# The norm chain of a two-block transformer: who sums the last squares, who takes the root, and how the result is spread

## The reference

```python
def rms_norm(x, g):
    xf = x.astype(jnp.float32)
    y = xf * lax.rsqrt(jnp.mean(xf * xf, axis=-1, keepdims=True) + EPS)
    return (y * g.astype(jnp.float32)).astype(x.dtype)
```

## Time and profile before

| what | us |
| --- | --- |
| runs | 2537.53, 2532.84, 2536.83 |
| profiled execution, its own time | 2532.73 |
| its span | 2530.9 |
| TensorE matmul busy | 2366.2 (93%) |
| VectorE busy | 1434.0 (57%) |
| ScalarE busy | 905.1 (36%) |
| GpSimd busy | 564.3 (22%) |
| mean granted clock of TensorE | 0.97 |

### The profile page before, as it was taken

The page is one execution under the profiler, slowest core; times in us unless marked ns, Lnnn a source line. Parts: engine busy times, 40 slices in busy tenths (PEclk is TensorE's granted clock), DMA queues, the critical chain, the costliest instruction groups (busy, mean ns, idle before and its releaser), DMA issues.

```text
span 2530.9 us, 29291 instructions
## 1 busy us (share of the span) xinstructions
PE 2366.2 (93%) x11174; PEld 1833.2 (72%) x11174; DVE 1434.0 (57%) x2277; ACT 905.1 (36%) x1539; POOL 564.3 (22%) x431
## 2 busy tenths in 40 slices
PE   6999999999998997888899999999899988999998
PEld 4665567888876864657788888888676566788886
DVE  4465547888757446665465566544636674534435
ACT  4244444232233223774332222222421773423232
POOL 2523114122211222002131211211123002322221
PEclk9999899999999999999899999999899999999999
DMA  5411114555521321001043334431122112222321
GB/s 185 150 53 42 55 34 175 200 179 188 175 79 34 107 67 52 27 22 47 30 133 123 127 128 132 127 103 62 50 89 83 34 34 67 84 92 92 102 90 50
DMA packets 77910, 234.06 MB, mean 92 GB/s; under 512 B 9215, under 2 KB 12416, under 8 KB 77772
## 3 DMA queue, kind: packets, MB, share of 16 engines
q1 hardware_dynamic: 70928, 217.48, 26.4%
q0 software_dynamic: 3520, 11.58, 1.3%
q10 hardware_dynamic: 3324, 3.14, 0.4%
HBM read 224.26 MB, written 7.90 MB: 92 GB/s over the span
## 4 chain that ended last, share of the span: by engine, by line
PE 86%; DVE 7%; ACT 3%; issue 2%; POOL 1%; ACTq 0%; DVEq 0%; POOLq 0%
PE psum L600 38%; PE psum L870 24%; PE psum L639 4%; PE psum L1168 3%; PE psum L1199 2%; PE psum L1125 2%; PE psum L659 2%; PE psum L1183 1%; PE psum L776 1%; PE psum L747 1%; PE psum L571 1%; PE psum L558 1%; PE psum L1139 1%; PE psum L1061 1%; DVE mla_stat L2007 1%
## 5 line engine op out<-in xcount | busy, mean ns | idle before, releaser
L600 PE MATMUL psum<-mix_split,weight_split 128*128 128x512 f32 x3792 | 786.7, 368 | 14.2 <-DVE mix_split L1316 5.9
L600 PEld LDWEIGHTS psum<-mix_split,weight_split 128*128 128x128 f32 x3792 | 651.0, 190 | 149.4 <-issue 17.7
L870 PE MATMUL psum<-hidden,weight_split 128*128 128x512 f32 (+1 forms) x3072 | 630.6, 366 | 0.0
L870 PEld LDWEIGHTS psum<-hidden,weight_split 128*128 128x128 f32 x3072 | 522.8, 188 | 104.4
L2086 ACT CAST weight_split<-weight_ring 128x1024 fp32r<-128x1024 f32 x269 | 276.8, 1040 | 301.2 <-PE psum L870 232.2
L2619 POOL TENSOR_TENSOR weight_split<-weight_ring,weight_split 128x1024 fp32r<-128x1024 f32 x89 | 233.9, 2628 | 541.3 <-ACT weight_split L2086 540.8
L1638 DVE TENSOR_TENSOR hidden<-hidden_tmp,hidden 128x512 fp32r<-128x512 f32 (+1 forms) x128 | 156.1, 1240 | 318.5 <-POOL hidden_tmp L2752 318.5
L2752 POOL TENSOR_TENSOR hidden_tmp<-hidden_tmp 128x512 f32<-128x512 f32 (+1 forms) x128 | 125.8, 994 | 615.1 <-ACT hidden L2331 614.9
L1262 DVE TENSOR_TENSOR weight_split<-weight_ring,weight_split 128x1024 fp32r<-128x1024 f32 x180 | 228.4, 1271 | 53.6 <-ACT weight_split L2086 53.6
L2327 ACT ACTIVATE hidden_tmp<-psum 128x512 f32<-128x512 f32 (+1 forms) x128 | 69.0, 539 | 494.9 <-PE psum L600 494.9
L600 PE MATMUL psum<-normed_in,weight_split 128*128 128x512 f32 (+1 forms) x1080 | 218.9, 364 | 9.0 <-DVE normed_in L1316 6.9
(11 more groups left out here) (303 smaller groups left out, 2415.6 us busy)
## 6 DMA issues: line engine op xcount, KB each, us to landing
weight_ring<-in_w_mlp SPq DMA_DIRECT2D x128, 512.0 KB, 3.8
weight_ring<-in_w_ff SPq DMA_DIRECT2D x64, 512.0 KB, 4.7
mod_ring<-in_w_mod SPq DMA_DIRECT2D x48, 512.0 KB, 3.8
late_ring<-in_w_mod SPq DMA_DIRECT2D x96, 256.0 KB, 3.5
weight_ring<-in_w_in SPq DMA_DIRECT2D x45, 512.0 KB, 3.7
weight_ring<-in_w_out SPq DMA_DIRECT2D x24, 512.0 KB, 3.6
weight_ring<-in_tables SPq DMA_DIRECT2D x13, 512.0 KB, 3.5
weight_ring<-in_w_v SPq DMA_DIRECT2D x8, 512.0 KB, 4.1
```

Of the source, the lines that this page charges most:

```text
L600: m = pe.matmul(psum[:, b + r, 0:hi - lo], w[:, part_w, :], x[:, part_x, k, lo:hi], start=k == 0 and part_w + part_x == 0, stop=k == KT - ...
L870: mm = pe.matmul(psum[:, b + r, 0:hi - lo], w[:, part_w, :], G[:, part_x, f % (2 * GROUP), lo:hi], start=jj == 0 and part_w + part_x == 0, ...
```

## The change

- The squares of the last tile are no longer added on VectorE. `column_sums` takes two matmuls for each 128 tokens, one on the sum of the first seven tiles and one on the last tile's squares, both into the same PSUM column. This holds for the norms in `LAST_APART`; `qn`, `kvn` and the context's part of `n3` sum as before.
- `mean` is gone: ScalarE's root reads the PSUM bank, with scale 1/n and EPS as bias. For `qn` the factor 1/sqrt(96) goes into scale and bias too.
- `diagonal` is gone: for each 128 tokens one matmul takes the column of inverses, repeated 128 times by an access pattern of step 0, as stationary operand, and the identity as moving one. The semaphore is raised after the fourth such matmul and after the last, and the first scaling of each range waits for its own.
- `n3` takes one root of ten columns: the product of the two norms' inverses is written as one root, of the gained mean plus EPS times the first mean plus EPS.
- ScalarE runs a root of one value where nothing waits (`root_table`), so that its table is loaded there.

The diff, without the edits that only pass the new arguments on:

```diff
+        LAST_APART = {"n1", "n2", "n3", "n3g", "l0n2", "l1n1", "l1n2", "fin"}
...
@@ -546,36 +549,43 @@
                 loads.append((name, index, width, split))
                 return i
-            def column_sums(tag, parts):
+            def column_sums(tag, parts, freed_by):
                 b = take()
                 bank_of[tag, "cols"] = b
                 wait_bank(b)
                 c = 0
-                for buf, lo, nt, name, key in parts:
-                    pe.wait_ge(*when(name, key))
+                for nt, planes in parts:
+                    for _, name, key in planes:
+                        pe.wait_ge(*when(name, key))
                     for t in range(nt):
-                        m = pe.matmul(psum[:, b, c:c + 1], buf[:, 0, lo + t * P:lo + (t + 1) * P], C["ones"][:, 0:1], start=True, stop=True)
-                        c += 1
+                        for n, (squares, _, _) in enumerate(planes):
+                            m = pe.matmul(psum[:, b, c + t:c + t + 1], squares[:, t * P:(t + 1) * P], C["ones"][:, 0:1], start=n == 0, stop=n == len(planes) - 1)
+                    c += nt
                 m.then_inc(*did(tag + "_pe", "cols"))
-                freed[b] = [(tag + "_vec", "mean")]
-            def on_all_partitions(tag, nt, diagonal=None, what="spread", diag="diag", n=2):
+                freed[b] = [freed_by]
+            def sums_and_last(tag, sums, last, lo, hi):
+                return (hi - lo) // P, [(sums[:, lo:hi], tag + "_vec", ("sum", KT - 2)), (last[:, lo:hi], tag + "_act", ("square", KT - 1))]
+            def on_all_partitions(tag, first, nt, what="spread", n=2):
                 b = take(n)
                 bank_of[tag, what] = b
                 wait_bank(*range(b, b + n))
-                pe.wait_ge(*when(tag + "_vec", diag))
-                src = SQ[:, 1, :] if diagonal is None else diagonal
-                for a in range(0, nt * P, 512):
-                    z = min(a + 512, nt * P)
-                    m = pe.matmul(bank(b, z, n)[:, a:z], C["ones"][:, :], src[:, a:z], start=True, stop=True)
-                m.then_inc(*did(tag + "_pe", what))
+                pe.wait_ge(*when(tag + "_vec", "inverse"))
+                for t in range(nt):
+                    m = pe.matmul(bank(b, nt * P, n)[:, t * P:(t + 1) * P], rs[:, first + t:first + t + 1].broadcast_to([P, P]), C["ident"][:, :], start=True, stop=True)
+                    if t % 4 == 3 or t == nt - 1:
+                        m.then_inc(*did(tag + "_pe", (what, t // 4)))
                 return b
-            def norm(tag, lo, nt, name, key, last):
-                column_sums(tag, [(SQ, lo, nt, name, key)])
-                b = on_all_partitions(tag, nt)
+            def norm(tag, nt, last, squares=None):
+                column_sums(tag, [sums_and_last(tag, SQ[:, 0, :], SQ[:, 1, :] if squares is None else squares, 0, nt * P)], (tag + "_act", "root"))
+                b = on_all_partitions(tag, 0, nt)
                 freed[b] = freed[b + 1] = [last]
             def product(tag, tiles, x, ranges, x_ready, evac, pool=None):
...
                     product("out1", [(i, ("w_out1", i))], HS_T1, X1, lambda k: (), lambda i, r: ("out1_vec", ("add", i, r)))
-                norm("n2", 0, 4, "n2_vec", ("sum", 7), ("n2_vec", ("scaled", 7, 0)))
+                norm("n2", 4, ("n2_vec", ("scaled", 7, 0)))
                 mlp("mlp1", lambda f: ("w_ff1", f), lambda g, m: ("w_ff2", (g, m)), HS_T1, G1, X1, "n2")
-                column_sums("n3", [(SQ, 0, 4, "n3_vec", ("sum", 7)), (squares_2, 0, 4, "n3g_vec", ("sum", 7)), (SQ, S, 2, "n3c_vec", ("sum", 7))])
-                b = on_all_partitions("n3", 6, diag="diag_both", what="both")
+                column_sums("n3", [sums_and_last("n3", SQ[:, 0, :], SQ[:, 1, :], 0, S), sums_and_last("n3g", squares_2[:, 0, :], squares_2[:, 1, :], 0, S),
+                                   (2, [(SQ[:, 0, S:T2], "n3c_vec", ("sum", KT - 1))])], ("n3_vec", "mean"))
+                b = on_all_partitions("n3", 4, 6, "both")
                 freed[b] = freed[b + 1] = [("n3_vec", ("scaled", 7, 1))]
-                b = on_all_partitions("n3", 4, SQ[:, 0, :], "final", "diag_final", 1)
+                b = on_all_partitions("n3", 0, 4, "final", 1)
...
@@ -1265,41 +1276,25 @@
                 split_lo(load_at[name, index] + AHEAD)
             def square_sum(tag, n, buf, tmp, a, z):
-                if n == 0:
+                if n == 0 or n == KT - 1 and tag in LAST_APART:
                     return
                 ve.wait_ge(*when(tag + "_act", ("square", n)))
                 if n > 1:
                     ve.wait_ge(*when(tag + "_vec", ("sum", n - 1)))
                 ve.tensor_tensor(buf[:, 0, a:z], buf[:, 0, a:z], tmp[:, a:z], ALU.add).then_inc(*did(tag + "_vec", ("sum", n)))
-            def mean(tag, nt, n):
-                ve.wait_ge(*when(tag + "_pe", "cols"))
-                ve.tensor_scalar(rs[:, 0:nt], psum[:, bank_of[tag, "cols"], 0:nt], 1.0 / n, EPS, ALU.mult, ALU.add).then_inc(*did(tag + "_vec", "mean"))
             def inverse(tag, nt):
                 ve.wait_ge(*when(tag + "_act", "root"))
                 ve.reciprocal(rs[:, 0:nt], rs[:, 0:nt]).then_inc(*did(tag + "_vec", "inverse"))
-            def diagonal(tag, dst, values, after, step="diag"):
-                nt = values.shape[1]
-                ve.wait_ge(*when(tag + "_vec", after))
-                ve.tensor_tensor(dst.rearrange("p (t q) -> p t q", q=P), C["ident"][:, :].unsqueeze(1).broadcast_to([P, nt, P]),
-                                 values.unsqueeze(2).broadcast_to([P, nt, P]), ALU.mult).then_inc(*did(tag + "_vec", step))
-            def spread_inverse(tag, nt, n):
-                mean(tag, nt, n)
-                inverse(tag, nt)
-                diagonal(tag, SQ[:, 1, 0:nt * P], rs[:, 0:nt], "inverse")
-            def normed_split(tag, HS, ranges, gain, shift, spread_bank, spread_steps):
+            def normed_split(tag, HS, ranges, gain, shift, what="spread"):
                 def scaled(t):
                     for r, (a, z) in enumerate(ranges):
-                        if t == 0 and r == 0:
...
+                        if t == 0:
+                            ve.wait_ge(*when(tag + "_pe", (what, r)))
...
@@ -1673,29 +1669,18 @@
             def between_blocks():
                 ve.wait_ge(*when("n3_pe", "cols"))
                 ps = psum[:, bank_of["n3", "cols"], :]
-                ve.tensor_scalar(rs[:, 0:4], ps[:, 0:4], 1.0 / D, EPS, ALU.mult, ALU.add).then_inc(*did("n3_vec", "mean_1"))
-                ve.wait_ge(*when("n3_act", "root_1"))
-                ve.reciprocal(rs[:, 0:4], rs[:, 0:4]).then_inc(*did("n3_vec", "inverse_1"))
-                ve.wait_ge(*when("n3_vec", "inverse_1"))
-                ve.tensor_tensor(rs[:, 4:8], ps[:, 4:8], rs[:, 0:4], ALU.mult).then_inc(*did("n3_vec", "gained_1"))
-                ve.wait_ge(*when("n3_vec", "gained_1"))
-                ve.tensor_tensor(rs[:, 4:8], rs[:, 4:8], rs[:, 0:4], ALU.mult).then_inc(*did("n3_vec", "gained_2"))
-                ve.wait_ge(*when("n3_vec", "gained_2"))
-                ve.tensor_scalar(rs[:, 4:8], rs[:, 4:8], 1.0 / D, EPS, ALU.mult, ALU.add).then_inc(*did("n3_vec", "gained_3"))
-                ve.tensor_scalar(rs[:, 8:10], ps[:, 8:10], 1.0 / D, EPS, ALU.mult, ALU.add).then_inc(*did("n3_vec", "mean"))
-                ve.wait_ge(*when("n3_act", "root_2"))
-                ve.reciprocal(rs[:, 4:10], rs[:, 4:10]).then_inc(*did("n3_vec", "inverse_2"))
-                ve.wait_ge(*when("n3_vec", "inverse_2"))
-                ve.tensor_tensor(rs[:, 4:8], rs[:, 4:8], rs[:, 0:4], ALU.mult).then_inc(*did("n3_vec", "inverse_both"))
-                diagonal("n3", SQ[:, 1, :], rs[:, 4:10], "inverse_both", "diag_both")
-                diagonal("n3", SQ[:, 0, 0:S], rs[:, 0:4], "inverse_both", "diag_final")
+                ve.tensor_scalar(rs[:, 0:4], ps[:, 0:4], D * EPS, None, ALU.add).then_inc(*did("n3_vec", "sums"))
+                ve.tensor_scalar(rs[:, 8:10], ps[:, 8:10], D * EPS, None, ALU.add).then_inc(*did("n3_vec", "sums_c"))
+                ve.wait_ge(*when("n3_vec", "sums"))
+                ve.scalar_tensor_tensor(out=rs[:, 4:8], in0=rs[:, 0:4], scalar=EPS, in1=ps[:, 4:8], op0=ALU.mult, op1=ALU.add).then_inc(*did("n3_vec", "mean"))
...
                     if i == 8:
-                        mean(f"qn{l}", nq, QL)
                         inverse(f"qn{l}", nq)
-                        ve.wait_ge(*when(f"qn{l}_vec", "inverse"))
-                        ve.tensor_scalar(rs[:, 0:nq], rs[:, 0:nq], 1.0 / math.sqrt(NOPE + ROPE), None, ALU.mult).then_inc(*did(f"qn{l}_vec", "scale"))
-                        diagonal(f"qn{l}", SQ[:, 1, 0:nq * P], rs[:, 0:nq], "scale")
                     if i == 10:
                         normed(f"qn{l}", [LAT[:, t, :] for t in range(3)], RG, lambda t: vec(f"qn_{l}", t))
                     if i == 11:
                         square_sum(f"kvn{l}", 1, SQ, SQF, 0, T2)
```

(18 more changed lines are left out.)

67 lines of the change are left out of this document (33 added, 34 removed).

## The result

| | before | changed |
|---|---|---|
| median of 15 runs, us | 2538.9 | 2523.66 |
| lowest and highest | 2532.47, 2542.24 | 2519.82, 2531.18 |
| ratio to before | 1 | 0.9946 [0.9936, 0.9957] |
| profiled execution, own time | 2532.73 | 2521.99 |
| its span and mean granted clock | 2530.9, 0.970 | 2520.1, 0.973 |

The changed kernel is faster by 0.54% by the ratio; the medians differ by 15.2 us, and the ratio is worth 13.7. The forecast was 4.6. It lies outside the predicted range (2525.5 to 2538) by 1.8.

What follows compares the result with a forecast made beforehand. The kernel was taken as a stream of matmuls that stands only where TensorE waits, as in the norms. Terms -2.2 - 2.5 - 1.5 + 0.9 + 0.7 = -4.6 us gave 2532 from the median 2536.83; range 2525.5 to 2538.

Steps and rivals of the forecast that it cites:

- The relay's links: Norms run as a relay without slack, in `n2` 0.02 to 0.14 us between instructions; a microsecond removed shortens the end equally.
- the queue of `n1`: In `n1` two weight casts, 1.98 us together, queue on ScalarE behind the root and shift with it; norm plus 0.9.
- The sum over the chains: Over seven norms, the time from squares to first scaling falls by 5.3 us in sum.
- The price of the second plane: Column sums read last squares from a second buffer: 16 passes for 8, 24 for 12; largest cost `n3`, plus 2.8 us.
- The base: Whole kernel: gain of 4.6 us taken from the median 2536.83, with the profiled execution 2532.73 lying 4.1 under it.
- The same gain from there: Whole kernel: the 4.6 us worked out on the profiled execution also holds from the median 2536.83, giving 2532.
- rival 2: Clock stays up through the norms' sums, -8.6 us or 2528; also through the spreads' first eight passes, -13; chance 0.12.
- 1: Clock falls before the sums in every norm: +0.9 us, no change, 2537.7; chance 0.18.
- 3: In the spread, a column read 128 times loads slower; at twice the half-clock price +15 us, 2552; chance 0.08.
- The page on wide and narrow: Cutting one spread into four costs 0.4 us more for each 512 columns, some 3 us of the gain over the chain.

Runs made afterwards that it cites:

- the kernel with the fuller fillers: Changed kernel plus thrown-away matmuls of 512 columns wherever TensorE stands in the seven norms; four executions of 2524 to 2532 us, two of 3987.11 and 3990.71.
- one-plane kernel: Changed kernel with the last add of squares back on VectorE, so the column sums read one buffer of squares; 2516.73 us, ratio 0.9916.
- two planes, half the filler: Changed kernel with both buffers of squares plus the halved thrown-away matmuls, four tiles fewer ahead of each sum from `n2` on; 2512.84 us, ratio 0.9896.
- one plane, half the filler: The one-plane kernel plus half as many thrown-away matmuls, ahead of the sums, between sums and spread and behind the spread; 2503.38 us, ratio 0.9874.

## Why the prediction was wrong

- *The relay's links.* Right, each within 0.1 to 0.2: starts 0.14 behind, passes at 0.12 and 0.22, eight passes of the spread at 2.0 at half clock, the first scaling after eight, the queue of `n1` (root at 21.92, casts behind it), `n3`. No link became late in its place. (In the prediction the sums of `n2` should end at 381.85 and not 381.88, which changes nothing.)
- *The sum over the chains.* -5.3 forecast, -5.2 measured, with a scatter of 4 us between profiles of the changed kernel. Within it `fin` gained 0.2 for 0.8: in two of three profiles the clock fell inside its 16 passes (2.37, 3.06), where before's eight were through in 1.02 each time. `n2` gained 0.3 more, as its spread began at the full clock.
- *The step that failed:* the sum ended at the first scaling, with nothing for the clock of what follows. The prediction said that the old spreads stood at 0.50 and priced half clock inside the chain, and then counted a microsecond of standstill as a microsecond of time. It is more. Across ten kernels timed and profiled, whose chains go from 37.1 to 62.3, the time follows the chain by 1.5 us for each (residuals up to 5 us; the kernel with the fuller fillers is left out, and with it the slope is the same). By that the 5.2 us of chain are worth 7.7. The measured 13.7 is 6 more: before lies 4.6 above the line and the changed kernel 2.2 below it. In the profiles the products behind the norms gave 1.4 us beyond the chains, and 5.2 lie in stretches that the sum had at zero, most of them chance by what the twelve profiles show. So the step that failed is known, and about half of what it missed is not accounted for.
- *The price of the second plane* was hidden in each norm's sum. Added up from the prediction's own terms it is 0.2 each in `n2` and `fin`, 0.4 in `l1n2`, 0.8 and 0.9 in the long norms, 2.8 in `n3` and 1.0 in `n1`: plus 6.3. The runs show 5.3 in the chains and 7 to 9 in the time. The loss would have been seen had the parts been summed over the norms, and not only the norms over the parts.
- *The base.* The profiled execution of before, 2532.73, lay 4.1 under the median shown; over 50 further executions of before on four chips the median is 2538.2, so it lay 5.4 under, and its clock of 0.970 over the mean of 0.9687. "The same gain from there" held for the chains only. The range ended 11.3 under the median shown, and so left out the outer end of its own rival 2, 13 under it, which is where the result came to lie.
- *Rivals.* 1 (the clock falls before the sums everywhere) is out: it had fallen before them in `n1` and, in two of three profiles, `n3` alone; in the others it fell within or behind them. 3 is out: 8 passes of the repeated column take 1.13 at the full clock, 0.14 each, as other narrow passes do. 2 had the direction right, and its outer end, minus 13, the size, for another reason, and so by luck: the clock stayed up through the sums in `n2` and once each in `l1n1` and `l1n2`, and through few spreads.
- *The page on wide and narrow.* By the Trainium skill, "TensorE: Matmul & The Clock Gate", section "Back-to-back issue gap", the cut into narrow passes was estimated to cost 3 us. No run has the wide form by itself. The run that has it is 12 to 14 us slower, for it brings the diagonal and the later release with it; the narrow passes' own price did not decide.

What stays open: where the 6 us lie that neither the chains nor the slope over the kernels accounts for. No run takes back the one root of `n3` or the earlier load of the root's table by itself.

## What to carry to other kernels

Where TensorE waits in a chain that the clock falls in, price a microsecond of chain above a microsecond of time; here it was about 1.5, over kernels whose chains differ by up to 25 us. Sum each part of a change over all places before judging the whole. An add of 0.69 us is not worth eight more one-column passes at either level of the clock: they take 0.98 at the full one and 1.8 at half. Releasing the first scaling as soon as its own passes of the spread are through was worth 6 to 8 us. Throwing matmuls into the standstills, sized to end just before the wait does, was worth nearly as much as the whole change (11 to 13 us on the one-plane kernel), but should be sized low and run many times. And one profile of a kernel whose executions differ by 10 us is no base for a change of 14.

## What the runs showed of the hardware

- With much thrown-away work in the standstills two of six executions ran at a granted clock of 0.554 throughout and took 3987 and 3991 us. None of the 4, 4 and 5 executions of the three kernels with half of it or less did; that is too few to call it safe.
- A column that is read 128 times as the stationary operand costs no more than any other: 8 passes in 1.13 at the full clock and 2.04 to 2.08 at half.
- Passes over one column behind dense matmuls run for a while at the full clock, 0.11 each from start to start, and the clock falls in or behind them. In `n3` it fell 1.2 us into a row of 36 (two planes, half the filler), 0.2 behind a row of 20 (one plane, half the filler) and 1.1 behind a row of 36 that took 4.07 (fuller fillers).
- ScalarE's root of 4 to 6 columns takes 0.26 to 0.27 from the bank for 0.20 from SBUF, and starts 0.04 to 0.05 behind TensorE's last pass.
- Between its first and its last matmul the long product from 1268 to 1787 us takes 519.17 in the changed kernel and all its variants and 517.53 in all four profiles of before, at the full clock throughout. That from 2175 to the last matmul takes 339.05 for 340.43, again to 0.02 in each profile, save for one variant that has before's time. No run here explains either.
